# The modulation of a quarter of X in two parts, in the two chunks behind the sums

## The reference, cut to what matters

```
mod = silu(c) @ w_ada + b_ada
shift1, scale1, gate1, shift2, scale2, gate2 = split(mod, 6)
h = rms_norm(x, norm1_w) * (1 + scale1) + shift1
proj = h @ w_in          # 2048 x 8192
```

## Time and profile before

| | |
|---|---|
| median of three runs | 2642.69 us |
| the profiled execution | 2648.83 us |
| its span in the trace | 2646.7 us |
| PE busy | 2530.5 us, 96% |
| DVE busy | 2026.1 us, 77% |
| ACT busy | 1296.1 us, 49% |
| DMA, mean over the span | 251 GB/s |
| chain that ended last | PE 77%, DVE 9%, DMA 5%, ACT 4% |

### The profile page before, as it was taken

The page is one execution under the profiler, slowest core; times in us unless marked ns, Lnnn a source line. Parts: engine busy times, 40 slices in busy tenths (PEclk is TensorE's granted clock), DMA queues, the critical chain, the costliest instruction groups (busy, mean ns, idle before and its releaser), DMA issues.

```text
span 2646.7 us, 32293 instructions
## 1 busy us (share of the span) xinstructions
PE 2530.5 (96%) x12265; PEld 2106.9 (80%) x12265; DVE 2026.1 (77%) x2308; ACT 1296.1 (49%) x1664; POOL 260.6 (10%) x321
## 2 busy tenths in 40 slices
PE   5999899999899999999998999999999999999998
PEld 4777777777788888888877788887788888888887
DVE  6778868898887888798898788875765566665566
ACT  4544485434454454445535554455455544544453
POOL 1000120202020110202020000450000000020000
PEclk9999999999999999999999999999999999999999
DMA  8898858998898979897967766454567777666654
GB/s 308 311 327 319 273 183 295 332 320 285 278 330 282 348 269 341 264 361 256 340 219 249 253 191 196 142 164 143 183 188 229 227 231 225 228 221 191 190 187 151
DMA packets 298362, 663.63 MB, mean 251 GB/s; under 512 B 20752, under 2 KB 21104, under 8 KB 297184
## 3 DMA queue, kind: packets, MB, share of 16 engines
q1 hardware_dynamic: 294976, 650.21, 72.8%
q0 software_dynamic: 2656, 9.66, 1.0%
q10 hardware_dynamic: 576, 1.70, 0.2%
HBM read 659.39 MB, written 2.10 MB: 250 GB/s over the span
## 4 chain that ended last, share of the span: by engine, by line
PE 77%; DVE 9%; DMA 5%; ACT 4%; issue 4%; SPq 0%; DVEq 0%; POOL 0%; ACTq 0%
PE PS L609 77%; DVE WL L1423 3%; DVE ACC L1431 2%; DMA RAW<-in_w_in 2%; ACT WH L1041 2%; DVE UQ L1423 1%; DMA RAW<-in_w_o 1%; DMA RAWX<-in_w_a_up 1%; DMA RAWX<-in_w_ada 1%; PE PS L612 0%; ACT L1041 0%; DMA RAWX<-in_w_in 0%; DVE acc L1423 0%; ACT UQ L1041 0%; ACT AH L1041 0%
## 5 line engine op out<-in xcount | busy, mean ns | idle before, releaser
L1041 ACT ACTIVATE WH<-RAW 128x1024 fp32r<-128x1024 f32 x567 | 600.1, 1059 | 803.9 <-PE PS L609 614.0
L1423 DVE TENSOR_TENSOR WL<-RAW,WH 128x1024 fp32r<-128x1024 f32 x567 | 705.2, 1245 | 361.7 <-ACT WH L1041 359.8
L609 PE MATMUL PS<-WH,AH 128*128 128x512 f32 x2052 | 817.9, 399 | 31.9 <-DVE WL L1423 17.3
L609 PE MATMUL PS<-WL,AH 128*128 128x512 f32 x2052 | 803.7, 392 | 0.0
L609 PE MATMUL PS<-WH,AL 128*128 128x512 f32 x2052 | 803.6, 392 | 0.0
L609 PE MATMUL PS<-HL,WH 128*128 128x512 f32 x2048 | 728.0, 400 | 8.4 <-issue 4.5
L609 PE MATMUL PS<-HL,WL 128*128 128x256 f32 x2048 | 576.7, 282 | 0.0
L609 PEld LDWEIGHTS PS<-WH,AH 128*128 128x128 f32 x2052 | 388.4, 189 | 126.3 <-DVE WL L1423 33.3
L609 PEld LDWEIGHTS PS<-HL,WH 128*128 128x128 f32 x2048 | 386.7, 189 | 106.4 <-issue 11.9
L609 PEld LDWEIGHTS PS<-WH,AL 128*128 128x128 f32 x2052 | 388.0, 189 | 83.0
L609 PEld LDWEIGHTS PS<-WL,AH 128*128 128x128 f32 x2052 | 388.6, 189 | 78.1 <-issue 1.0
(11 more groups left out here) (241 smaller groups left out, 1959.2 us busy)
## 6 DMA issues: line engine op xcount, KB each, us to landing
RAW<-in_w_ff SPq DMA_DIRECT2D x335, 512.0 KB, 4.3
RAW<-in_w_ada SPq DMA_DIRECT2D x284, 512.0 KB, 5.0
RAW<-in_w_in SPq DMA_DIRECT2D x192, 512.0 KB, 4.6
RAWX<-in_w_ada SPq DMA_DIRECT2D x100, 512.0 KB, 5.3
RAWY<-in_w_ff SPq DMA_DIRECT2D x96, 512.0 KB, 4.1
RAWX<-in_w_ff SPq DMA_DIRECT2D x81, 512.0 KB, 5.2
RAWX<-in_w_in SPq DMA_DIRECT2D x48, 512.0 KB, 5.2
RAW<-in_w_out SPq DMA_DIRECT2D x32, 512.0 KB, 3.6
```

The costliest lines, as they stand in the source:

```text
L609: return e.matmul(o, l, r, start=start, stop=stop, skip_group_check=True)
L1041: return e.activation(o, i, f, **kw)
L1423: return e.tensor_tensor(o, a, b, op)
```

## The change

In each of the quarters 1 to 3 ACT's eight instructions are cut into two parts of four (two k-tiles). They stood in the chunk of the sums (21, 41, 61), ahead of `evac`; they stand now in the two chunks behind it (22 and 23, 42 and 43, 62 and 63), behind `evac`. DVE's four instructions of `quarter_low` stood in the chunk of the sums; they stand now by two in the second and third chunk behind it (23 and 24, 43 and 44, 63 and 64), still between `feed` and `evac`. Quarter 0, DVE's `quarter`, the order of the transfers that SP issues and the order on PE are as before.

```
-            def quarter(q):
+            def quarter(q, part, parts):
                 e.wait_ge(s_mod, 3 * q + 3)
-                for k in range(4 * q, 4 * q + 4):
+                n = 4 // parts
+                for k in range(4 * q + n * part, 4 * q + n * part + n):
...
                 feed(j + look(j))
-                if j in SUMS[1:]:
-                    quarter(SUMS.index(j))
...
                 for q, t in bl.ended(j):
                     evac(q, t)
+                for q in range(1, 4):
+
+                    if 0 <= j - SUMS[q] - 1 < 2:
+                        quarter(q, j - SUMS[q] - 1, 2)
...
-            def quarter_low(q):
-                for k in range(4 * q, 4 * q + 4):
+            def quarter_low(q, part, parts):
+                n = 4 // parts
+                for k in range(4 * q + n * part, 4 * q + n * part + n):
...
                     feed(j + look(j))
-                    if j in SUMS[1:]:
-                        quarter_low(SUMS.index(j))
+                    for q in range(1, 4):
+                        if 0 <= j - SUMS[q] - 2 < 2:
+                            quarter_low(q, j - SUMS[q] - 2, 2)
```

More of the change, by code:

```diff
@@ L1404, in _ @@
                     feed(0)
-                    quarter(0)
+                    quarter(0, 0, 1)
                 feed(j + look(j))
-                if j in SUMS[1:]:
-                    quarter(SUMS.index(j))
                 for q, t in bl.ended(j - 1):
@@ L1967, in _ @@
                     feed(0)
-                    quarter_low(0)
+                    quarter_low(0, 0, 1)
                 if j in norms:
```

## The result

| | before | changed |
|---|---|---|
| median (14 runs each, side by side) | 2644.45 us | 2637.57 us |
| lowest to highest | 2641.21 to 2650.95 | 2632.00 to 2640.59 |
| profiled execution | 2648.83 us | 2636.26 us |
| its span | 2646.7 us | 2634.2 us |

The ratio is 0.9967 with a 95% interval of 0.9959 to 0.9976: faster by 8.7 us (6.3 to 10.8). The means of the 14 runs differ by as much (8.6 us), the two medians by only 6.9 us. Forecast were 9.5 us and 2633.2 us, in a range of 2628.5 to 2640; the measured median lies in it, 4.4 us above the forecast.

What follows compares the result with a forecast made beforehand. PE, busy 96% of the span, was taken to bound the kernel; only its waits and slow matmuls count. Gains 6.0 + 0.3 + 3.2 = 9.5 us, so 2642.7 - 9.5 = 2633.2 us, range 2628.5 to 2640.

Steps and rivals of the forecast that it cites:

- Place 1, the order of ACT and DVE: Chunk 21: SG emptied at 105.1, PE's 3.69 us wait goes, chunks 23 to 27 ready 0.5 to 1.5 us early.
- Place 1, the clock: Behind chunk 22's wait: the clock stays high, so 2.3 us of slow matmuls go too; 6.0 us gained with the wait.
- 3.7 (clock falls anyway): Lower bound of the gain at chunk 21: 3.7 us, if PE's clock still falls there.
- Place 2, the wait for AL: Before chunk 44: PE's 1.25 us wait for WL becomes a wait for AL of some 1.75 us.
- Place 2, the transfers: Near chunk 50: weights about 2 us late behind POOL's two transfers; with the AL wait 3.75 us, gain 0.3.
- about 3 us are spare: Weights near chunk 50: slot freed 9.1 us ahead, less ACT's 1.5 us lead and a 4.6 us landing.
- the burst: POOL's two transfers (1.84 MB) near chunk 44: 4.8 us of all DMA engines at 386 GB/s, pushing back later weights.
- Place 3: Chunk 61 on: waits of 0.35, 0.3 and 0.5 us, cost 1.15 instead of 4.4; gain 3.2 us, bounds 1.5 and 4.4.
- Supply: Rival: without PE's pauses the ring cannot refill, transfer waits return at chunks 21 and 61; gain 3.5 us, 2639.2; chance 0.12.
- The clock falling anyway: Rival: lower clock still comes, from the sums' matmuls or new waits; gain 5.6 us, 2637.1; chance 0.13.
- AL behind the weights: Rival: late weights of chunks 45 and 65 delay AL; 2655; slower once landings are over about 4 us late; chance 0.03.
- Gain given back later: Rival: gain lost at the pool branch (260 to 340 us), or the bank wait only moves; 2642.7; chance 0.06.

Runs made afterwards that it cites:

- places23: Kernel before with the new order in quarters 2 and 3 only, quarter 1 as before; median 2640.67 us, ratio 0.9980.
- low_early: Changed kernel with DVE's AL one chunk earlier (22 and 23, 42 and 43, 62 and 63); median 2636.31 us, ratio 0.9965.
- evac_first: Kernel before with ACT's eight modulation instructions behind the emptying in the same chunk, unsplit, DVE's AL unmoved; median 2641.24 us, ratio 0.9984.
- burst_early: Changed kernel with POOL's two transfers let go at 8 k-tiles of AL, not 12; median 2642.03 us, ratio 0.9979.
- burst_first_low_early: Changed kernel with POOL's two transfers let go at 4 k-tiles of AL and DVE's AL one chunk earlier; median 2637.63 us, ratio 0.9962.
- burst_parted: Changed kernel with PM sent at 4 k-tiles of AL, WP at 12, AL one chunk earlier in quarters 1 and 2; median 2632.06 us, ratio 0.9956.
- changed once more: Changed kernel run again with nothing altered; 2636.12 us (one run).
- burst_late: Changed kernel with POOL's two transfers let go when all 16 k-tiles of AL are made; median 2639.86 us, ratio 0.9973.
- no_split: Changed kernel with ACT's quarter in one piece of eight instructions in the first chunk behind the sums; median 2640.41 us, ratio 0.9984.
- before_again: Kernel before, run once more with nothing altered; 2646.01 us (one run).

## Why the prediction was right

*Place 1, the order of ACT and DVE.* Every step stood. SG was expected at 105.1 and came at 104.67 in a trace that runs 0.38 us ahead; the two parts, the roundings and the WL came within 0.3 us of the list, and PE had no wait.

*Place 1, the clock.* "The 2.3 us go too" was true of this pair of traces and too much as a forecast for the medians: places23 has the wait without the slow stretch. The sure part is 4.0 us. The bound "3.7 (clock falls anyway)" was the right number with the wrong reason: the clock doesn't fall anyway in the changed kernel, it sometimes doesn't fall in the kernel before.

*Place 2, the wait for AL.* Forecast 1.75 us before chunk 44, measured 1.80, ended by DVE AL. The wait changed its name as told.

*Place 2, the transfers.* Mis-sized: 2.0 us forecast, 0.39 (0.79 in the second trace) measured, so the gain there was 2.2 and not 0.3. The failed step is "about 3 us are spare". It counted when ACT would like to have the weights. ACT did wait, 5.02 us:

```profile
180.04 1.06 ACT L1041 ACTIVATE WH<-RAW 128x1024 fp32r<-128x1024 f32 x1 [1.66 <-PE PS L609]
186.13 1.06 ACT L1041 ACTIVATE WH<-RAWX 128x1024 fp32r<-128x1024 f32 x1 [5.02 <-DMA RAWX<-in_w_in]
```

Of the 5.02 us it stands 1.66 before each chunk at this pace anyway, until PE frees a buffer, so the weights were 3.4 us late for ACT, not 2. But with three buffers of WH and WL, ACT works some two chunks (5.4 us) ahead of PE. Less the 2.2 us of its own and DVE's work 3.2 are left, which the forecast did not count, so PE felt 0.39. low_early then showed that part of this cover is the AL wait itself: without it PE stands 1.90 us for weights. (The 386 GB/s taken for the burst is not the best stretch of its rows, 403 is; the burst is 4.6 us by that and not 4.8, which changes little.)

*Place 3.* Forecast 1.15 us of waits in three pieces, measured 0.38 in one, before chunk 64. The other two, 0.3 and 0.5, came from adding up DVE's steps end to end. Gain 4.3 for 3.2, but part of it is clock: 1.5 to 1.8 us behind the UQ wait (the kernel before takes 42.0 us from the sums to the first matmul of the pool branch; evac_first, with nearly the same waits and the clock up, takes 40.2), and 0.65 us that the forecast did not see. It lies behind that first matmul (before, then changed):

```profile
270.55 2.83 PE L609 MATMUL PS<-PT,G 128*128 128x256 f32 x8 [1.93 <-ACT PT L1041]
```

```profile
257.92 1.99 PE L609 MATMUL PS<-PT,G 128*128 128x256 f32 x8 [1.90 <-ACT PT L1041]
```

From this matmul to the rounding for chunk 80 it is 25.6 to 25.7 us in six of the fourteen traces (both of the kernel before, evac_first, burst_early, burst_first_low_early, burst_parted), where the clock fell, and 24.9 to 25.0 in the other eight. That leaves 1.9 us of place 3 for the order alone.

*The sum.* 12.9 us by the traces, 9.5 forecast, 8.7 (6.3 to 10.8) in the ratio. That 9.5 comes so near is luck in part: 2.3 us of clock at place 1 were counted in full, and 1.9 us at place 2 were missed. The median itself came out 4.4 us above the forecast one, 1.8 of it because the three runs that the forecast started from (2642.69) lay under the median of all 14 (2644.45). The trace of the kernel before was a dear one at places 1 and 3 and a cheap one later: around chunk 567 PE stands three times in both kernels (0.94, 1.08 and then 2.81 us before, 0.94, 1.08 and 2.66 now), and in the changed kernel the clock falls behind the second of them and again behind the third, which costs 3 us:

```profile
1806.00:1816.00 10.00, 7.34 (x23) 5.61 (x22) 2.01 (x3) 1.79 (x3) 0.00 (x0) 0.71 0.35 121
```

```profile
1819.00:1829.00 10.00, 6.47 (x29) 5.12 (x30) 2.67 (x5) 1.92 (x4) 0.00 (x0) 1.00 0.44 155
```

(first the changed kernel, then the one before, at nearly the same matmuls). From the rounding for chunk 565 to that for 568 it is 17.35 us in four of the fourteen traces (before, changed once more, low_early, burst_late) and 20.3 to 21.3 us in the other ten. Taking 4.0 + 2.2 + 1.9 for the parts that don't hang on the clock, 8.1 us would be left, which is near the measured 8.7. That is an argument from few traces, not shown. The forecast's last sign against itself was a distance between the traces that is smaller at the end: it was 13.3 us at the rounding for chunk 80 and 12.5 at the end. By the rows above this is the clock around chunk 567, and not gain given back by the kernel's waits.

*The rivals.* Supply: no. The stretch from 125 to 135 us moved 383 GB/s with PE at full pace; the trace does not agree with the 358 GB/s of the Trainium skill, "DMA: Bandwidth & Descriptors", section "Bandwidth", as the forecast read it. The same section gives that figure for a core while the other core of its pair streams too, and here one core ran alone. The clock falling anyway: not at these places. AL behind the weights: PE's waits before chunks 44 and 64 were 1.80 and 0.38 us in both traces of the changed kernel, so the weights of 45 and 65 were there in time. Its threshold was worked out wrong: with its own terms, 2 x (1.75 + x + 2.3) + 4.8 reaches 14.4 at x = 0.75 us (at 3.05 if the clock stays up), not at about 4. Gain given back later: none before chunk 560 in this pair of traces, then 3 us by the clock.

## What to carry to other kernels

Work that nobody needs yet belongs behind the emptying of a bank that somebody needs next, and in pieces no longer than the slack of what follows; here no instruction was shortened, and the order alone was worth 4.0 us at place 1. Before pricing a late transfer, follow it through all buffers to the engine at the end: its first reader may wait 5 us and the last engine 0.4. And when one of two neighbouring waits is removed, try the other alone and both together: here either one hid the other.

## What the runs showed of the hardware

TensorE's granted clock after a wait is not set by the length of the wait alone. Behind 3.69 us of idle it fell to its lower level (1.2 GHz of 2.4) in two traces of the kernel before and stayed up in places23. Near 2 us there are pairs at either level: behind 2.35 us it fell and behind 2.34 us it stayed in one and the same trace (no_split),

```profile
173.00:178.00 5.00, 4.86 (x21) 4.05 (x22) 4.59 (x7) 1.06 (x1) 1.49 (x2) 1.00 0.99 338
233.00:238.00 5.00, 5.00 (x16) 3.93 (x16) 4.73 (x6) 0.58 (x1) 0.00 (x0) 0.66 0.93 307
```

and in the same wait for UQ at place 3 it fell behind 1.89 us (before_again, 0.66 from 244 to 249) and stayed behind 1.88 (evac_first, 1.00 from 240 to 245):

```profile
243.75 0.50 PE L609 MATMUL PS<-WH,AH 128*128 128x512 f32 x1 [1.89 <-DVE UQ L1423]
```

```profile
239.46 0.50 PE L609 MATMUL PS<-WH,AH 128*128 128x512 f32 x1 [1.88 <-DVE UQ L1424]
```

Behind 1.90 us it fell in low_early; behind 1.81 (places23) and 1.64 (burst_parted) it stayed. Behind the 1.90 to 1.94 us before the pool branch it fell in six traces and stayed up in seven (in the fourteenth the wait was 0.94); around chunk 566, behind the same 1.08 us, it fell in ten and stayed up in four. The loss was 0.65 us at the pool branch, 1.6 to 2.4 at the three places, and 3 to 4 around chunk 566. That may be a good part of the 3 to 13 us between the fastest and the slowest run of one kernel here (the runs without a trace can't show it), and it is a reason to trust a difference of single traces only place by place.

A wait of TensorE is also time for the DMA engines: at place 2 the 1.8 us for AL carried most of a burst of 1.84 MB that alone left PE waiting for 1.9 us.
